# First FFN of a two-block kernel: the low half of every fourth weight chunk made by ScalarE and an adding GpSimd DMA

## What is computed

```python
D_MODEL = 2048
SEQ = 256
D_FF = -(-8 * D_MODEL // (3 * 256)) * 256
...
        h = h + mixed @ w_out[l]

        hn = rmsnorm(h, ffn_norm[l])
        h = h + (jax.nn.silu(hn @ w_gate[l]) * (hn @ w_up[l])) @ w_down[l]
    return rmsnorm(h, final_norm)
```

## Time and profile before

| | |
|---|---|
| time, median of 3 runs | 2521.89 us (2519.06 to 2522.16) |
| the profiled execution: its span, first to last instruction | 2517.6 us |
| what the median of the runs is above that span | 4.3 us |
| TensorE busy | 2480.8 us, 99% |
| VectorE busy | 1378.9 us, 55% |
| ScalarE busy | 1231.0 us, 49% |
| GpSimd busy | 46.7 us, 2% |
| moved by DMA | 459.45 MB, 182 GB/s in the mean |
| mean granted TensorE clock | 0.996 |

### The profile page before, as it was taken

How to read it: one execution, slowest core, us unless ns; L and a number is a source line. 1 busy time by engine, 2 the same in 40 slices (tenths; PEclk the granted TensorE clock), 3 DMA queues, 4 the chain that set the end, 5 groups by cost and what they waited for, 6 DMA issues and landing times.

```text
span 2517.6 us, 30756 instructions
## 1 busy us (share of the span) xinstructions
PE 2480.8 (99%) x11388; PEld 2060.0 (82%) x11388; DVE 1378.9 (55%) x1634; ACT 1231.0 (49%) x1521; POOL 46.7 (2%) x96
## 2 busy tenths in 40 slices
PE   8999999999999999999999999999999999999998
PEld 6888888888888888888888778877888888888886
DVE  5455555655454544554445587565565555555444
ACT  5446555445444444444445455564555554544443
POOL 1000100000000000000002000000000000000000
PEclk9999999999999999999999999999999999999999
DMA  7655555666666666666666445555556566566564
GB/s 221 193 177 155 177 152 161 197 200 194 197 191 184 193 185 191 191 185 191 191 191 207 143 150 156 163 185 183 164 178 192 176 192 189 171 197 205 189 195 147
DMA packets 239475, 459.45 MB, mean 182 GB/s; under 512 B 16550, under 2 KB 18768, under 8 KB 239008
## 3 DMA queue, kind: packets, MB, share of 16 engines
q1 hardware_dynamic: 237680, 452.65, 59.3%
q0 software_dynamic: 1680, 5.69, 0.7%
q10 hardware_dynamic: 32, 0.01, 0.0%
HBM read 456.19 MB, written 2.10 MB: 182 GB/s over the span
## 4 chain that ended last, share of the span: by engine, by line
PE 97%; ACT 1%; DVE 1%; issue 1%; DMA 0%; DVEq 0%; ACTq 0%
PE acc L514 31%; PE acc L516 30%; PE acc L515 30%; PE mis L487 1%; PE mis L863 1%; PE mis L567 1%; PE mis L775 1%; DVE lo L1339 0%; PE mis L556 0%; ACT hi L899 0%; PE mis L588 0%; PE mis L597 0%; PE mis L570 0%; DMA xin<-in_x 0%; DVE xa_lo L1366 0%
## 5 line engine op out<-in xcount | busy, mean ns | idle before, releaser
L1339 DVE TENSOR_TENSOR lo<-raw,hi 128x1024 fp32r<-128x1024 f32 x858 | 1040.1, 1222 | 912.0 <-ACT hi L899 910.3
L899 ACT ACTIVATE hi<-raw 128x1024 fp32r<-128x1024 f32 x858 | 894.9, 1056 | 826.5 <-PE acc L516 813.3
L514 PE MATMUL acc<-hi,xb_hi 128*128 128x512 f32 x1920 | 755.7, 394 | 6.0 <-DVE lo L1339 4.4
L516 PE MATMUL acc<-hi,xb_lo 128*128 128x512 f32 x1920 | 748.4, 390 | 0.0
L515 PE MATMUL acc<-lo,xb_hi 128*128 128x512 f32 x1920 | 747.8, 389 | 0.0
L514 PEld LDWEIGHTS acc<-hi,xb_hi 128*128 128x128 f32 x1920 | 360.9, 188 | 85.4 <-DVE lo L1339 9.8
L516 PEld LDWEIGHTS acc<-hi,xb_lo 128*128 128x128 f32 x1920 | 360.7, 188 | 75.8
L515 PEld LDWEIGHTS acc<-lo,xb_hi 128*128 128x128 f32 x1920 | 361.1, 188 | 73.2
L514 PE MATMUL acc<-hi,xa_hi 128*128 128x512 f32 (+1 forms) x768 | 301.0, 392 | 7.1 <-DVE lo L1339 5.5
L516 PE MATMUL acc<-hi,xa_lo 128*128 128x512 f32 (+1 forms) x768 | 297.2, 387 | 0.0
L515 PE MATMUL acc<-lo,xa_hi 128*128 128x512 f32 (+1 forms) x768 | 296.9, 387 | 0.0
(11 more groups left out here) (301 smaller groups left out, 1132.5 us busy)
## 6 DMA issues: line engine op xcount, KB each, us to landing
raw<-in_w_in SPq DMA_DIRECT2D x216, 512.0 KB, 4.2
raw<-in_w_ffn_in SPq DMA_DIRECT2D x176, 512.0 KB, 4.5
raw<-in_w_gate SPq DMA_DIRECT2D x88, 512.0 KB, 4.4
raw<-in_w_up SPq DMA_DIRECT2D x88, 512.0 KB, 4.3
raw<-in_w_down SPq DMA_DIRECT2D x88, 512.0 KB, 4.2
raw<-in_w_ffn_out SPq DMA_DIRECT2D x88, 512.0 KB, 4.2
raw<-in_w_out SPq DMA_DIRECT2D x32, 512.0 KB, 4.4
raw<-in_w_o SPq DMA_DIRECT2D x32, 512.0 KB, 4.3
```

Of the source, the lines that this page charges most:

```text
L514: nc.tensor.matmul(o, xh, wh, start=kb == 0, stop=False)
L516: last = nc.tensor.matmul(o, xl, wh, start=False, stop=kb == k - 1)
L899: nc.scalar.activation(hi[:, slot, :, 0:width], raw[:, slot, :, 0:width], ACT.Copy)\
L1339: V.tensor_tensor(lo[:, slot, :, 0:width], raw[:, slot, :, 0:width], hi[:, slot, :, 0:width].bitcast(F32), ALU.subtract).then_inc(lo_ready, 1)
```

## The change

The change concerns the chunks of the first FFN in slot 3, 44 of 176 (`by_dma`). For these, ScalarE makes a second copy after the high half: lo = -raw, through `scale=-1.0` (`neg_ready`). GpSimd waits for it and starts a DMA from `raw` to `lo` that adds (`accum_op=ALU.add`). VectorE does no subtraction for them, only an instruction that counts up `lo_ready`. TensorE waits for the landing of that DMA (`lo_added`, 16 for each) in place of `lo_ready`, and so does the load queue before it loads the slot anew, and once before the down projection.

The copy reads `raw` again, but `lo` is of the matmul's type, so what it writes is rounded as `hi` was: it is minus hi. The DMA then adds raw in float32, and lo is raw - hi as before.

```diff
+ADD_EVERY, ADD_SLOT = 4, 3
...
+        def added(n, c):
+
+            k = (n.start + c + 1) // ADD_EVERY - PH["ffn"][0] // ADD_EVERY
+            return Count(16 * k, n.i, 16 * n.per // ADD_EVERY).at(0)
+
+        def by_dma(phase, n, c):
+
+            return phase == "ffn" and (n.start + c) % RING == ADD_SLOT
...
-            def load(n, c, src):
+            def load(n, c, src, phase=None):
 
                 slot = (n.start + c) % RING
-                if n.low(c) >= RING:
+                if by_dma(phase, n, c) and n.low(c) - RING >= PH["ffn"][0]:
+                    sp.wait_ge(lo_added, added(n, c - RING))
+                elif n.low(c) >= RING:
                     sp.wait_ge(lo_ready, n.at(c - RING + 1))
...
             couple("ffn", w_gate, w_up, 0, 0, KD, FT)
+            sp.wait_ge(lo_added, 16 * (2 * FT * KD // CK // ADD_EVERY))
             plain("down", w_down, 0, KF, 2)
...
-                    pe.wait_ge(lo_ready, n.at(c0 + c + 1))
+                    if by_dma(phase, n, c0 + c):
+                        pe.wait_ge(lo_added, added(n, c0 + c))
+                    else:
+                        pe.wait_ge(lo_ready, n.at(c0 + c + 1))
...
                 nc.scalar.activation(hi[:, slot, :, 0:width], raw[:, slot, :, 0:width], ACT.Copy)\
                     .then_inc(hi_ready, 1)
+                if by_dma(phase, n, c):
+                    nc.scalar.activation(lo[:, slot, :, :], raw[:, slot, :, :], ACT.Copy, scale=-1.0)\
+                        .then_inc(neg_ready, 1)
...
                 slot = (n.start + c) % RING
+                if by_dma(phase, n, c):
+                    V.engine_nop().then_inc(lo_ready, 1)
+                    return
                 dve.wait_ge(hi_ready, n.at(c + 1))
...
+            for k in range(2 * FT * KD // CK // ADD_EVERY):
+                pool.wait_ge(neg_ready, k + 1)
+                pool.dma_start(lo[:, ADD_SLOT, :, :], raw[:, ADD_SLOT, :, :], accum_op=ALU.add).then_inc(lo_added, 16)
+
             pool.wait_ge(chunk_used, PH["in2a"][0])
             pool.dma_start(gfbc[:, :], a["final_norm"].partition_broadcast(P)).then_inc(gbc_in, 16)
```

More of the change, by code:

```diff
@@ L291, in two_blocks @@
         chunk_used = sem("chunk_used")
+        neg_ready = sem("neg_ready")
+        lo_added = sem("lo_added")
         acc_free = [sem(f"acc_free{j}") for j in range(2)]
@@ L414, in load, with tile @@
                 sp.dma_start(raw[:, slot, :, 0:w], src).then_inc(raw_in[slot], 16)
-            def tile(n, c0, w, col, k, width=W):
+            def tile(n, c0, w, col, k, width=W, phase=None):
                 for c in range(k // CK):
-                    load(n, c0 + c, w[:, CK * c:CK * c + CK, ds(col, width)])
+                    load(n, c0 + c, w[:, CK * c:CK * c + CK, ds(col, width)], phase)
             def plain(phase, w, col, k, n_pairs):
@@ L439, in couple @@
                     n = Count(n0, i, per)
-                    tile(n, 0, w1, col1 + i * W, k)
-                    tile(n, k // CK, w2, col2 + i * W, k)
+                    tile(n, 0, w1, col1 + i * W, k, phase=phase)
+                    tile(n, k // CK, w2, col2 + i * W, k, phase=phase)
             plain("qkv", w_in, 0, KD, 3)
@@ L489, in turn, with tile @@
                 last.then_inc(turned, 1)
-            def tile(n, c0, k, x, tile_no, par, width=W, k0=0, sides=None, hook=None, beside=None):
+            def tile(n, c0, k, x, tile_no, par, width=W, k0=0, sides=None, hook=None, beside=None, phase=None):
                 for c in range(k // CK):
@@ L542, in couple @@
                              sides=sides if j == 0 else None,
-                             hook={4: lambda: hooks(i)} if hooks and j == 0 else None)
+                             hook={4: lambda: hooks(i)} if hooks and j == 0 else None, phase=phase)
             def attention_steps(g, first, head0, b, q, k, v, rope, diff, values_in=None):
@@ L891, in _, with split @@
                 .then_inc(att_in, 16)
-            def split(n, c, width=W):
+            def split(n, c, width=W, phase=None):
                 slot = (n.start + c) % RING
@@ L1126, in _ @@
                                                  scale=rs_h[:, t:t + 1]).then_inc(acc_free[t0 % 2], 1)
-                    split(n, c)
+                    split(n, c, phase="ffn")
             n0, t0, i3, per = PH["down"]
```

## The result

The changed kernel takes 2524.7 us (2522.07 to 2528.62, 20 runs) against 2520.16 us (2519.06 to 2522.16, 20 runs) for the one before. The ratio is 1.0019, with a 95% interval of 1.0012 to 1.0025: slower by 4.5 us, not by the 100 forecast, and far under the range. The forecast started from 2522, the median of three runs; twenty runs give 2520.16, so its base was 1.7 us too high, which does not matter beside 100.

A forecast was written before the change was run, and what follows sets the result against it. TensorE was taken to bound the kernel, so freed VectorE time and added work counted 0. Slot 3's turn, 13.39 us against 11.11, lost 2.28 in 44 turns: 2522 + 100 = 2622 us, range 2550 to 2800.

The forecast's parts named there:

- The loop of slot 3: First FFN: load, two copies, four hops and A make 13.39 us against TensorE's 11.11 per ring turn; 100 us lost.
- the second condition: First FFN: from slot release to TensorE's need is 8.16 us, so A may be 5.9; called the weaker limit.
- A: Slot 3, first FFN: time from the end of the negated copy to the addition's landing; taken as 6.8 us.
- The bound from below: Slot 3's addition: if paid like the quick 1 MB load, A is 5.2 us.
- the likeliest case's own range: Whole kernel: 2552 us (A = 5.2) to 2737 us (A = 9.4), for the forecast given 0.62.
- the four hops: Slot 3's loop: four hops between engines, 0.12 us together, counted beside A.
- the threshold at 4.52: Slot 3's loop, 6.59 us + A, exceeds TensorE's 11.11 us turn once A is over 4.52 us.
- The rival "hidden": First FFN: the addition is hidden and the kernel not slower, 2522 us, if A is under 4.52; chance 0.12.
- argument by slope: Slot 3's addition: the small load's 3.9 us, with the quick 1 MB load adding 1.3, gives 4.6 for 512 KB.
- The collision: DMA engines, first FFN: a delayed load stretches the addition by 1.8 us, A 8.6, time 2701 us; chance 0.16.
- the fit that was set aside: GpSimd's DMA: 2.0 us plus bytes at 436 GB/s gives 4.4 us for 1 MB of reads, which would hide.
- the prediction had feared more: First FFN: each TensorE gap brings about 10 us at half clock, 2842 us in all; chance 0.08.

The follow-up runs named there:

- e1: Changed kernel without the 44 adding DMAs and their waits; ScalarE's second copy stays and VectorE subtracts as before; 2520.23 us, ratio 1.0001 to the kernel before.
- e2: Changed kernel with the 44 DMAs only copying raw to lo within SBUF, adding nothing; 2521.33 us, ratio 1.0003 to the kernel before.
- e3: Changed kernel with one GpSimd fill of 128x1024 words before each addition, delaying it 1.01 us; 2555.38 us, ratio 1.0144 to the kernel before.
- e4: Changed kernel with three GpSimd fills of 128x1024 words before each addition; 2649.73 us, ratio 1.0511 to the kernel before.
- e10: Changed kernel with one GpSimd fill of 128x256 words before each addition, delaying it 0.4 us; 2532.06 us, ratio 1.0044 to the kernel before.
- e5: Changed kernel with two alternating raw buffers for slot 3, so its load no longer waits for the addition; 2524.18 us, ratio 1.0015 to the kernel before.
- e7: Changed kernel with a 512 KB load of x from HBM into lo in place of each addition; 2521.49 us, ratio 1.0004 to the kernel before.
- e9: Changed kernel with chunks 1 and 5 of the first pair of tiles back on VectorE, 42 additions left; 2521.07 us, ratio 1.0005 to the kernel before.
- e8: The changed kernel again, unaltered, for a second profile; 2522.41 us in one run.
- e6: Changed kernel with additions for slots 1 and 3, 88 chunks in place of 44; 2620.89 us, ratio 1.0385 to the kernel before.

## Why the prediction was wrong

**What bounds the kernel.** Right: TensorE, with nothing to gain from VectorE. e1 shows that ScalarE's copy costs nothing, and e2, where VectorE's 44 subtractions are gone and the landing is quick, that their loss gives nothing.

**The loop of slot 3.** Right as a mechanism. e3, e4 and e10 moved the addition by known amounts, and the time followed about one for one above a threshold; the second condition, from release to need, did not set the pace in any of them. e5 took the loop away, and ScalarE's waits for loads went with it, and so did every loss behind the first pair of tiles.

**The size of A.** This is the step that failed: "I start from the load of the same size, 5.0, and add a second read of 0.52 MB at the rate of the busy engines, 190 / 0.65 = 292 GB/s, 1.8 us: A = 6.8." Measured from the same point it is 0.30 + 4.5 = 4.8 in the turn above. Both halves were too long. A copy within SBUF takes 3.5 us (e2), while the row taken as base was a load from HBM, among other loads; one of that size takes 4.3 in the FFN (e7). And the second read adds 1.1 us (e2), not 1.8. The bound from below, 5.2, failed with it, since it too was built from loads from HBM alone. That excluded what happened from the likeliest case's own range, and the overall range began at 2550. Both bounds also stood on single loads: the two of 1 MB that took 5.2 and 7.6 us take 6.5 and 6.8 in the trace of the changed kernel.

**The other terms.** The load was put at 4.35 us, the median of loads that run beside each other. The load of slot 3 is issued when the addition has landed, so it meets idle engines (a DMA share of 0.02 from 715.5 to 716.5 us in the turn above): 3.85. The two copies overlap, 2.01 in place of 2.12. GpSimd's hop, 0.30, was missing as such and is counted in A. In sum the loop is 10.66 in place of 13.39, against 11.11. Of the 2.73 us too many, 2.0 are A, 0.6 the load and copies, and 0.12 the four hops counted beside A. With the threshold at 4.52 as the prediction had it, even the measured A of 4.8 would have cost 0.28 × 44 = 12 us; the corrected terms put it at 11.11 − 3.85 − 2.01 = 5.25, and by e3's slack of 0.25 to 0.30 it is about 5.1.

**The rival "hidden".** It came true but for 4.5 us, with 0.12 given to it, and not by its own condition: it asked for A under 4.52, and A is 4.8. Its argument by slope gives 4.5 us for 512 KB, not 4.6, and leans on the 32 KB load of 3.9 us; in the same trace sixteen loads of 0.5 to 22 KB took 4.9 to 5.9. That an addition lands after 4.6 us is therefore no success of that slope. Its price of nothing missed the start: the FFN's first pair of tiles has less slack than the average one. ScalarE comes late there, since the residual's side work lies before chunk 4, and three high halves follow at once. Chunk 5's addition then runs beside the loads that catch up, 5.6 us instead of 4.5. The prediction divided the FFN evenly and read typical turns, not the first. e9 shows that the two additions at the start cost most of it; that it is the late copy and the meeting with loads is read from the trace. The price also missed that with so little slack a settled turn is late now and then (e8).

**The collision.** It shows where loads catch up (622 to 626 us, share 1.09; e5) and with twice the additions (e6). In the settled turn read above, the load queue's wait for the addition keeps the two apart: from 712.5 to 714.5 us the additions' queue has 85.1% of the engines and the loads' 2.5%. The prediction counted that wait only as a cost. But it saves little there: with the wait gone (e5) a settled addition takes 0.2 us longer, not the 1.8 of that rival.

**The second read, and the fit that was set aside.** The Trainium skill, "Collectives: The Full Stack", section "The bandwidth ceiling", says that a reducing DMA pays for two source reads. The share bears it out, 24.6% against 13.0% for the copy. The Trainium skill, "DMA: Bandwidth & Descriptors", section "Anatomy of one DMA — SWDGE (gpsimd) path", fits 2.0 us plus the bytes at 436 GB/s; as an estimate that is 3.2 us for 512 KB and, with two reads, 4.4. Measured were 3.5 for the copy and 4.6 for the addition. The prediction had set the fit aside for the 5.0 of a load from HBM beside other loads; for these transfers within SBUF it is 0.2 to 0.3 short.

**Not settled.** How the 4.5 us divide between waits and clock varies with the run: the FFN cost 2.0 and 3.3 us in two profiles, and one fall of the clock outside it cost 1.4 in one of them. Why single additions in settled turns land late (5.8 us with the engines nearly idle at its end) stays open. The changed kernel's runs spread over 6.5 us and those of before over 3.1, which fits waits that come in some executions and not in others.

## What to carry to other kernels

When a new transfer enters a ring, add up the loop that its slot must pass before it can be loaded again, and compare it with the ring's turn; here it was that sum, not the engines' shares, that told the cost. Take each term from a row with the same source, the same path and the same company: a median over transfers that run side by side is too long for one that is issued alone. Then look at the first turn by itself, since a loop that fits with 0.3 us to spare on average fails where an engine comes late, and now and then in a settled turn too.

## What was not expected of the hardware

- GpSimd's DMA within SBUF of 512 KB lands after 3.5 us, with addition after 4.6; issuing one takes 530 and 857 ns on GpSimd. From HBM the same size took 4.3 in the same place and 5.0 earlier.
- After the same TensorE gap of 2.0 us near 1428 the clock fell for 3.4 us in one profile and not in another of the same kernel. In e4, gaps of 2.6 us every 13.8 us mostly left it at 1.00 (mean 0.97 from 640 to 1080 us), where the prediction had feared more; in e10 a single gap of 3.44 us was followed by 4 us at 0.50.
